# First block of a two-block sequence model on one core: residual held with tokens on partitions, down products that move 512 weight columns, norms by an accumulator and a diagonal matmul

## The reference, cut to what matters

```python
def rmsnorm(x, w):
    xf = x.astype(jnp.float32)
    y = xf * lax.rsqrt(jnp.mean(xf * xf, axis=-1, keepdims=True) + EPS)
    return (y * w.astype(jnp.float32)).astype(x.dtype)

def first_block(x, ...):
    for i in range(DEPTH):                       # DEPTH = 2
        h = rmsnorm(x, norm_mix_pre[i])
        m = ssd_mixer(h, ...) if i == 0 else rglru_mixer(h, ...)    # both end in  y @ w_out (+ b_out)
        x = x + rmsnorm(m, norm_mix_post[i])
        h = rmsnorm(x, norm_ffn_pre[i])
        f = conv_ffn(h, ...)                     # ends in  (gelu(g) * v) @ w_down
        x = x + rmsnorm(f, norm_ffn_post[i])
    return x

def second_block(x, c, ...):
    for l in range(DEPTH):
        h = rms_norm(x, norm1_g[l]) * (1.0 + sc1) + sh1
        ...                                      # attention and delta-rule branches, gates, mlp
```

## Time and profile before

| what | value |
| --- | --- |
| time, median of 3 runs | 1887.17 us (1887.06 to 1896.51) |
| profiled execution, its own time | 1896.59 us |
| its span, first to last instruction | 1894.7 us |
| PE busy, weight loads busy | 96%, 91% of the span |
| DVE busy, ACT busy | 69%, 54% |
| mean granted clock of PE | 0.982 of full speed |

### The profile page before, as it was taken

One profiled execution on the slowest core, in us unless ns is written; L12 is line 12 of the kernel. 1 busy time (PEld: TensorE's weight loads), 2 busy tenths in 40 slices (PEclk: granted clock), 3 DMA queues, 4 the chain that ended last, 5 costly groups with the idle time before them and its releaser, 6 DMA issues. The chain is left out here.

```text
span 1894.7 us, 39895 instructions
## 1 busy us (share of the span) xinstructions
PE 1815.2 (96%) x16265; PEld 1721.7 (91%) x16265; DVE 1316.4 (69%) x2054; ACT 1017.5 (54%) x1542; POOL 29.5 (2%) x48
## 2 busy tenths in 40 slices
PE   6999989999989989999989999999998999999999
PEld 5997879999979979999979998989998999999999
DVE  5857777777778887777767767765557776676554
ACT  5645465555566755555547555454445665454443
POOL 0000000000000000000000001000000000100000
PEclk8999999999999999999989999999999999999999
DMA  7440457667665556656734340345553442044553
GB/s 294 178 177 1 156 184 252 253 263 270 250 255 179 206 181 212 245 227 216 276 110 156 134 156 3 116 153 199 191 187 132 156 150 96 22 158 156 186 191 111
DMA packets 43895, 333.63 MB, mean 176 GB/s; under 512 B 4865, under 2 KB 4993, under 8 KB 5633
## 3 DMA queue, kind: packets, MB, share of 16 engines
q1 hardware_dynamic: 38592, 277.89, 40.7%
q0 software_dynamic: 4608, 50.33, 7.2%
q10 hardware_dynamic: 576, 3.71, 0.5%
HBM read 330.86 MB, written 1.05 MB: 175 GB/s over the span
## 5 line engine op out<-in xcount | busy, mean ns | idle before, releaser
L522 DVE TENSOR_TENSOR w_lo<-raw,w_hi 128x1024 fp32r<-128x1024 f32 x526 | 639.8, 1224 | 389.3 <-ACT w_hi L513 379.3
L513 ACT ACTIVATE w_hi<-raw 128x1024 fp32r<-128x1024 f32 x526 | 554.8, 1060 | 591.7 <-PE unit L544 375.9
L542 PE MATMUL unit<-h_hi,w_hi 128*128 128x256 f32 x2656 | 753.3, 284 | 35.8 <-DVE h_lo L426 14.8
L543 PE MATMUL unit<-h_lo,w_hi 128*128 128x256 f32 x2656 | 745.6, 281 | 0.0
L544 PE MATMUL unit<-h_hi,w_lo 128*128 128x256 f32 x2656 | 745.4, 281 | 0.0
L542 PEld LDWEIGHTS unit<-h_hi,w_hi 128*128 128x128 f32 x2656 | 508.6, 191 | 47.4 <-issue 33.5
L544 PEld LDWEIGHTS unit<-h_hi,w_lo 128*128 128x128 f32 x2656 | 508.3, 191 | 0.0
L543 PEld LDWEIGHTS unit<-h_lo,w_hi 128*128 128x128 f32 x2656 | 507.2, 191 | 0.2
L542 PE MATMUL acc<-mv_hi,w_hi 128*128 128x256 f32 x1360 | 382.3, 281 | 5.9 <-DVE mv_lo L600 3.3
L543 PE MATMUL acc<-mv_lo,w_hi 128*128 128x256 f32 x1360 | 379.1, 279 | 0.0
L544 PE MATMUL acc<-mv_hi,w_lo 128*128 128x256 f32 x1360 | 379.0, 279 | 0.0
(11 more groups left out here) (388 smaller groups left out, 1721.9 us busy)
## 6 DMA issues: line engine op xcount, KB each, us to landing
raw<-w_in SPq DMA_DIRECT2D x263, 1024.0 KB, 4.8
ada_ring<-ada_in POOLq DMA_DIRECT2D x32, 1536.0 KB, 7.5
keep<-gates_in ACTq DMA_DIRECT2D x1, 1280.0 KB, 6.3
par<-par_in ACTq DMA_DIRECT2D x1, 1261.0 KB, 14.5
x<-x_in SPq DMA_DIRECT2D x1, 1024.0 KB, 5.5
out<-x SPq DMA_DIRECT2D x4, 256.0 KB, 2.1
con<-con_in ACTq DMA_DIRECT2D x1, 950.0 KB, 4.9
con<-con_in ACTq DMA_DIRECT2D x1, 130.0 KB, 5.7
```

What stands on the lines that cost most here:

```text
L513: act(half(w_hi, c, k), raw[c % RAW][:, CW // 2 * k:CW // 2 * (k + 1)], ACT.Copy).then_inc(S("high_parts"), 1)
L522: tt(half(w_lo, c, k), raw[c % RAW][:, CW // 2 * k:CW // 2 * (k + 1)], half(w_hi, c, k).bitcast(f32), ALU.subtract).then_inc(S("chunk_spli ...
L542: mm(out, w, m, start=first, stop=False)
L543: mm(out, w, ml, start=False, stop=False)
```

## The change

In the first block `x` is held with 128 tokens on each partition set: `xt` is 2 halves of 128 tokens x 1024 features in the same memory. The down products swap operands: the activations `mv_hi`, `mv_lo` are stationary, 512 weight columns move, and each of the four `acc` banks holds 128 tokens x 512 features (`pe_tokens_down`, 24 matmuls of 512 columns per chunk). The closing chunk runs bank by bank. A norm's sum of squares is then a sum along the free axis, taken by ACT's accumulator output as it squares (`act_post`, `act_pre`); root and scale are one number per partition. The weights of the post norms come as rows, broadcast over partitions, by five DMAs on ACT's queue (`act_rows`) into the unused `h`. To return to features on partitions, DVE scales an identity matrix by the root (`dve_diag`) and PE multiplies 128 x 128 blocks of `xt` by it (`pe_turn`), which turns and scales at once; ACT and DVE make `h_hi` and `h_lo` out of PSUM (`act_turned`, `dve_turned`), or, where `h` itself is needed, by way of it (`dve_turned_exact`). The two blocks of the other product stand together behind the update of the first 128 tokens (`pe_gap`). In the second block's first stage 16 transposes put `x` back to features on partitions. The second block is otherwise unchanged.

```diff
+        def act_post(ac, stage):
+            ...
+            ac.preload_act_table_set(LN_EXP)
+            for b in range(4):
+                m = b // 2
+                if biased:
+                    ac.wait_ge(S("lru_m"), b + 1)
+                else:
+                    closed(ac, stage, b)
+                s = slice(512 * b, 512 * (b + 1))
+                act(spare[:, s], source[:, s], ACT.Square, accum_out=stat(k, 3 * m + b % 2)).then_inc(S("norm_steps"), 1)
+                if b % 2:
+                    ...
+                    act(total, total, ACT.Ln, bias=stat(k, 3 * m + 2), scale=1.0 / D).then_inc(S("norm_steps"), 1)
+                    ac.wait_ge(S("norm_steps"), post_step(k, SUM_AT[b] + 1))
+                    act(total, total, ACT.Exp, scale=-0.5).then_inc(S("norm_steps"), 1)
+
+        def act_pre(ac, name, ready):
+            n = PRE[name]
+            for m in range(2):
+                ready(m)
+                act(spare[:, 1024 * m:1024 * (m + 1)], xt[:, m, :], ACT.Square, accum_out=stat(n, 6 + m)
+                    ).then_inc(S("norm_steps"), 1)
+                ...                       # Ln and Exp on 128x1
+
+        def dve_post(dve, link, stage):
+            ...
+            def product(b):
+                ...
+                if biased:
+                    closed(dve, stage, b)
+                    source = flat(R["m"])[:, 512 * b:512 * (b + 1)]
+                    tt(source, accb[b], rowb(1, b), ALU.add).then_inc(S("lru_m"), 1)
+                    dve.wait_ge(S("lru_m"), b + 1)
+                else:
+                    dve.wait_ge(S("norm_steps"), post_step(k, SUM_AT[b]))
+                ...                       # mw[:, b] = source * weight row; one 128x1 step if b is even
+            def update(b):
+                s = xt[:, b // 2, 512 * (b % 2):512 * (b % 2 + 1)]
+                return stt(s, mw[:, b, :], stat(k, 3 * (b // 2) + 1), s, ALU.mult, ALU.add)
+            product(0)
+            product(1)
+            dve.wait_ge(S("norm_steps"), post_step(k, 4))
+            update(0)
+            update(1).then_inc(S("xt_ready"), 1)
+            product(2)
+            product(3)
+            dve.wait_ge(S("norm_steps"), post_step(k, 8))
+            update(2)
+            update(3).then_inc(S("xt_ready"), 1)
+
+        def dve_diag(dve, name):
+            n = PRE[name]
+            for m in range(2):
+                dve.wait_ge(S("norm_steps"), pre_step(n, 3 * m + 3))
+                ts(diag[:, m, :], ident, stat(n, 6 + m), None, ALU.mult).then_inc(S("norm_factors"), 1)
+
+        def pe_turn(pe, name, n0):
+            ...
+            for m in range(2):
+                pe.wait_ge(S("norm_factors"), 4 * n + m + 1)
+                for t in range(8):
+                    ins = mm(turned(banks, t)[:, P * m:P * (m + 1)], xt[:, m, P * t:P * (t + 1)], diag[:, m, :],
+                             start=True, stop=True, skip_group_check=True)
+                    if m == 1 and t % 2:
+                        ins.then_inc(S("turned"), 1)
+
+        def act_turned(ac, name, n0, weight):
+            ...
+                    ins = act(h_hi[:, t, :], turned(banks, t), ACT.Identity, bias=one("zero"), scale=weight(t))
+        def dve_turned(dve, name, n0, weight):
+            ...
+                    ins = stt(h_lo[:, t, :], turned(banks, t), weight(t), h_hi[:, t, :].bitcast(f32),
+                              ALU.mult, ALU.subtract)
+
+        def pe_tokens_down(pe, c, b, first, last, i=None, chunks=0, downs=0, closing=False):
+            pe.wait_ge(S("mv_ready"), at(i, downs, b + 1))
+            def product(k, m, n, begin, end):
+                s, e = slice(P * m, P * (m + 1)), slice(512 * n, 512 * (n + 1))
+                return three(accb[2 * m + n], mv_hi[:, b % 2, k, s], mv_lo[:, b % 2, k, s], half(w_hi, c, k)[:, e],
+                             half(w_lo, c, k)[:, e], begin, end)
+            if closing:
+                pe.wait_ge(S("chunk_split"), at(i, 2 * chunks, 2 * c + 2))
+                for m in range(2):
+                    for n in range(2):
+                        product(0, m, n, False, False)
+                        ins = product(1, m, n, False, True)
+                        if (m, n) != (1, 1):
+                            ins.then_inc(S("bank_closed"), 1)
+                ins.then_inc(S("half_done"), 2)
+                return
+            ...
 
-        def pe_gap(pe, first, second):
+        def pe_gap(pe, stage, second, name, n0):
 
             n = GAP[second]
-            pe_norm(pe, first)
...
-            pe_ada(pe, n, misc[1])
-
-        def pe_gap_end(pe, second):
-            pe_ada(pe, GAP[second] + 1, accb[0])
+            x_updated(pe, stage)(0)
+            pe_ada(pe, n, accb[0])
+            pe_ada(pe, n + 1, accb[1])
+            pe_turn(pe, name, n0)
...
+            def act_between(stage, name, second, weight):
+                act_post(ac, stage)
+                act_pre(ac, name, x_updated(ac, stage))
+                ahead(act_half, ac, END[stage] - 1, 0)
+                act_turned(ac, name, U0[second], weight)
+                ahead(act_half, ac, END[stage] - 1, 1)
...
+            def dve_between(stage, name, second, weight):
+                dve_post(dve, link, stage)
+                dve_diag(dve, name)
+                dve_turned(dve, name, U0[second], weight)
+                ahead(dve_split, dve, END[stage] - 1)
```

More of the change, by code:

```diff
@@ L398, in pe_norm @@
             n = NI[name]
[L399 to L404 removed]
+            for q in range(4):
+                pe.wait_ge(S("squares"), 4 * n + q + 1)
                 for t in (2 * q, 2 * q + 1):
[L406 removed]
+                    last = mm(misc[0][:, 0:T], ones, h[:, t, :], start=(t == 0), stop=(t == 7))
             last.then_inc(S("square_sums"), 1)
[L409 to L412 removed]
         def x_ready(eng, name):
@@ new lines, in build, with post_step @@
+        rowb = lambda r, b: rows[:, r, 512 * (b % 2):512 * (b % 2 + 1)]
+        spare = flat(h_hi[:, :, :])
+        POST = {"ssd_out": 0, "ffn0": 1, "lru_out": 2, "ffn1": 3}
+        ROWS = {"ssd_out": 0, "ffn0": 1, "lru_out": 2, "lru_bias": 3, "ffn1": 4}
+        SIDE = {"ssd_out": 1, "ffn0": 2, "gates": 3, "lru_out": 5, "ffn1": 6}
+        PRE = {"mix_pre0": 0, "ffn_pre0": 1, "mix_pre1": 2, "ffn_pre1": 3, "pre1_0": 4}
+        STEPS = 8 + 6
+        def post_step(k, j):
+            return 6 + STEPS * k + j
@@ new lines, in pre_step, with stat, act_rows, turned_banks @@
+        def pre_step(n, j):
+            return STEPS * n + j
+        SUM_AT = (1, 2, 5, 6)
+        def stat(n, k):
+            return sums[:, n % 2, k:k + 1]
+        def act_rows(ac, stage):
+            r = 1 if stage == "lru_bias" else 0
+            ac.dma_start(rows[:, r, :], rows_in[:, ROWS[stage], :]).then_inc(S("side_loads"), 16)
+        def turned_banks(n0):
+            return [unit[n0 % 2], unit[(n0 + 1) % 2], misc[0], misc[1]]
+        def turned(banks, t):
+            return banks[t // 2][:, T * (t % 2):T * (t % 2 + 1)]
@@ L466, in dve_post @@
+        def act_turned(ac, name, n0, weight):
+            banks = turned_banks(n0)
             for q in range(4):
-                dve.wait_ge(S("squares"), 4 * NI[name] + q + 1)
+                ac.wait_ge(S("turned"), 4 * PRE[name] + q + 1)
                 for t in (2 * q, 2 * q + 1):
-                    ins = ts(source[:, t, :], source[:, t, :], weight(t), None, ALU.mult)
-                if q == 1 and name in ADDED:
-                    dve_squares(dve, name)
-            link(ins)
-            ahead(dve_half, dve, END[stage] - 1, 0)
@@ L592, in pe_down @@
                 ins.then_inc(S("half_done"), 1)
+        def pe_tokens_down(pe, c, b, first, last, i=None, chunks=0, downs=0, closing=False):
[14 more added lines that the diff above has]
+                return
+            for k in range(2):
+                pe.wait_ge(S("chunk_split"), at(i, 2 * chunks, 2 * c + k + 1))
+                for m in range(2):
+                    for n in range(2):
+                        ins = product(k, m, n, first and k == 0, False)
+                ins.then_inc(S("half_done"), 1)
         def act_moving(ac, b, src, i=None, downs=0):
@@ L906, in act_ssd @@
             rms(1)
+            act_rows(ac, "ssd_out")
             act_out(ac, "ssd_out", ssd_pair, normed, all_ahead=False)
@@ L1385, in act_lru @@
             moving(1)
+            act_rows(ac, "lru_out")
             mult(3)
@@ L1470, in dve_lru @@
             ahead(dve_split, dve, c0 + 13)
-            for t in range(8):
-                if t % 2 == 0:
-                    closed(dve, "lru_out", t // 2)
-                ins = ts(R["m"][:, t, :], acc8[:, t, :], pr("b_out", t), None, ALU.add)
-                if t % 2:
-                    ins.then_inc(S("lru_m"), 1)
         def ada_load(pool, s, block):
@@ L1637, in pe_b2_in @@
                 pe_unit(pe, c0 + j, n0 + j)
+                if l == 0 and j == 1:
+                    pe.wait_ge(S("ada_turned"), 32)
```

(9 more changed lines are left out.)

217 lines of the change are left out of this document (120 added, 97 removed).

## The result

The changed kernel takes 1898.29 us, the median of 15 runs (1893.03 to 1903.37), beside 1887.74 us for the kernel before in the same comparison (15 runs, 1885.65 to 1896.51). The ratio is 1.0044, with a 95% interval of 1.003 to 1.0059. The forecast was 1858. The change was meant to move about 29 us out of the program; it moved some 10 us in.

What follows compares the result with a forecast made beforehand. PE bounds the stages of products; a chain over ACT, PE and DVE, with DVE nearly full, bounds the four passages. -8.5 - 21.8 - 1.0 + 2.0 = -29.3 on the median 1887.2 gave 1858 us, range 1842 to 1880.

Steps and rivals of the forecast that it cites:

- the part on the down products: In `ffn0`, `ffn1` and `ssd_out`, one 512-column matmul at 0.220 us replaces two narrow ones: -8.5 us.
- fixed part: In each down matmul, a cost paid once whatever its width, beside streaming: about 0.006 to 0.010 us, taken as 0.006.
- The rival with 0.28: Down products: a 512-column matmul costs 0.28 us, so the kernel gets slower, 1922 us; chance 0.06.
- The passages: Four stretches from last down to first up matmul get shorter: -5.3, -6.45, -2.8 and -7.2, sum -21.8 us.
- ACT's half split: In the passages, queued between last root and first turned tile: an added wait, in the first from 5.5 to 6.6 us.
- hand-offs: In the passages, passing work between engines and a possibly halved clock: 0.8 us added, 0.9 behind `lru_out`.
- a passage above 13 us: Sign in the profile after: a passage that stays above 13 us would show the forecast wrong.
- Behind `lru_out`: Passage to `ffn1`: DVE free only at 0.75 us, updates end at 10.5, passage 16.45 in place of 19.26: -2.8.
- The first 24 up matmuls: Start of the up stage after a passage: slow before and counted unchanged.
- rival 3: Whole kernel, more than forecast: wide matmuls at 0.215 us and PE kept at upper clock, 1848 or 1843 us; chance 0.20.
- The ends: Program start, from parameters to last tile of `h`: -1.0 us; second block's first stage, 16 transposes: +2.0 us.
- The sum: Whole kernel: down products, passages and ends together, -29.3 us.

Runs made afterwards that it cites:

- the first experiment: Changed kernel with its weight tiles put back to the addresses of the kernel before (padding 76 columns instead of 84); 1867.2 us, ratio 0.9883.
- the second: Kernel before with its weight tiles alone moved by 32 bytes (padding 92 columns instead of 84); 1930.07 us, ratio 1.0225.
- 256 bytes less: Changed kernel with its weight tiles 256 bytes below their place in the kernel before (padding 12 columns); 1866.21 us, ratio 0.9880.
- place 192: Changed kernel with its weight tiles 128 bytes below their place in the kernel before (padding 44 columns); 1891.83 us, ratio 1.0013.

## Why the prediction was wrong

**The step that failed** is in the part on the down products: "the columns that stream are the same, so only what is paid once per matmul can go", with "about 0.006 to 0.010" left per matmul, and with it the unspoken rest of the sum, that every other matmul keeps its spacing. The 0.113 and 0.118 of the earlier trace rows are not streaming and a fixed part: both occur for the same matmul at the same place of the weights, and the spacing changes with where the weights lie against the activations. Behind its first two chunks the stage shown above has 0.1133 before and 0.1187 after. The change moved the weights by 32 bytes. That costs about 30 us (1.0044 less 0.9883, of 1888), spread over the 11,544 matmuls of both blocks that read the weight tiles; the first experiment takes it away and the second brings it into the old kernel. The view that would have warned was at hand: the padding tile ahead of the weights, whose width no part of the change adjusted, though it adds and shortens tiles ahead of it. The range had no room for it, since no rival let a matmul that isn't edited run slower.

**The down products** were sized wrongly apart from that. With the weights in the good place a wide matmul takes 0.229 us on the average, not 0.220. With the pauses between chunks left out, two narrow ones took 0.2273 in `ffn0`, 0.2267 in `ffn1` and 0.2352 in `ssd_out`; a wide one takes 0.2292, 0.2292 and 0.2291. So nothing is gained in place of 8.5 us: `ssd_out` gives 1.2 and the other two take back 1.7. In the kernel as changed, at 0.2333 to 0.2335, they lose 4.6. The term that failed is the fixed part. It rests on the estimate that 256 columns stream in 0.1075, which no run shows; the lowest level seen for such matmuls is 0.1133. Measured against twice that estimate, 0.215, a wide matmul has 0.014 too much and two narrow ones at the lower level 0.012: what is left is not paid once per matmul. The rival with 0.28 is refuted; what else the row holds was not looked into.

**The passages** were right as a sum and in their shape: 9.35, 9.35, 16.45 and 9.75 forecast, 8.71, 8.70, 14.55 and 9.33 measured, 25.4 us in place of 21.8. The chain of the first, in the timeline of the kernel after (start us, duration us):

```profile
241.53 0.60 ACT L502 ACTIVATE h_hi<-acc 128x512 fp32r<-128x512 f32 x1 [0.71 <-PE acc L689]
...
242.00 1.41 DVE L549 TENSOR_TENSOR keep<-acc,h 128x512 f32<-128x512 f32 x2
...
243.44 1.42 DVE L553 SCALAR_TENSOR_TENSOR x<-keep,sums,x 128x512 f32<-128x512 f32 x2
...
244.89 1.06 ACT L516 ACTIVATE h_hi<-x 128x1024 fp32r<-128x1024 f32 x1 [0.45 <-DVE x L553]
...
246.17 1.06 PE L581 MATMUL misc<-rstd,x 128*128 128x128 f32 x8
...
246.40 0.20 ACT L521 ACTIVATE sums<-sums 128x1 f32<-128x1 f32 x1
...
246.50 1.04 ACT L658 ACTIVATE w_hi<-raw 128x1024 fp32r<-128x1024 f32 x1
246.63 0.29 DVE L571 TENSOR_SCALAR rstd<-con,sums 128x128 f32<-128x128 f32 x1 [1.58 <-ACT sums L521]
...
247.06 1.07 PE L581 MATMUL unit<-rstd,x 128*128 128x128 f32 x8
...
247.72 1.93 ACT L592 ACTIVATE h_hi<-unit,con,par 128x256 fp32r<-128x256 f32 x4 [0.18 <-PE unit L581]
...
248.78 1.79 DVE L601 SCALAR_TENSOR_TENSOR h_lo<-unit,par,h_hi 128x256 fp32r<-128x256 f32 x4 [1.86 <-ACT h_hi L592]
```

The last down matmul starts at 241.09. DVE is last at the updates, which end at 244.86, 3.8 after it; 3.9 was forecast. The second root comes at 246.6, 5.5 after, as forecast. From there the prediction had two paths side by side, the identity and the turn to 6.45 and ACT's half split to 6.6, and let the split be last. Measured, the split ends at 247.54, 6.45 after the last down matmul, and the first turned tile can be read at 247.72, 6.63 after: PE is last, by 0.18, and the split is not a wait that is added. PE begins with the second 128 tokens at 247.06, 0.14 after DVE has their identity (246.92) and just as it is through with the first. So the time of this point was right and the engine that sets it was not, in what is nearly a tie. From there to the up stage the trace has 2.08 where 1.95 was counted. The sum without hand-offs, 8.55, comes close to the 8.71 measured; the 0.8 added for hand-offs, which no row gave, was 0.64 too much. (That a passage above 13 us would show the forecast wrong cannot be meant for the one behind `lru_out`, which it put at 16.45.)

Behind `lru_out` DVE came free before the last down matmul, not 0.75 after it as in the earlier trace rows. In the kernel after (start us, duration us):

```profile
651.38 2.35 DVE L667 TENSOR_TENSOR w_lo<-raw,w_hi 128x1024 fp32r<-128x1024 f32 x2
...
662.60 1.42 DVE L553 SCALAR_TENSOR_TENSOR x<-keep,sums,x 128x512 f32<-128x512 f32 x2 [0.78 <-ACT sums L509]
```

That split ends at 653.73, 0.84 before the last matmul, so the updates end 9.45 after it and not 10.5, which is 1.05 of the 1.9 us. From the updates to the up stage the trace has 5.1 and the prediction 5.0 without its hand-offs; the 0.9 that it added for these was again not needed.

**The first 24 up matmuls** were counted unchanged. They gained 6.0 us, for the most part by the clock, as rival 3 had half expected. The windows of the 24 behind the first passage, in the kernel before and then in the kernel after, where the granted clock is the last number but two:

```profile
259.20:264.00 4.80, 4.63 (x24) 4.43 (x25) 4.67 (x8) 1.26 (x2) 0.00 (x0) 0.64 0.75 307
```

```profile
249.80:253.20 3.40, 3.40 (x24) 3.04 (x25) 3.33 (x7) 2.62 (x5) 0.00 (x0) 1.00 0.96 404
```

Before, PE had stood or done small sums for 15 us and began the stage mostly at 1.2 GHz; now its pause is shorter and it begins at 2.4 GHz. Behind all four passages the clock went from 0.55 to 0.70 up to 1.00.

**The ends** came out nearly right, by luck in the first part. The last down matmul of `ssd_out` starts 4.3 us earlier with the weights put back, where 1.0 for the start and 3.1 for the down products had been counted; but the first up matmul of the program already starts 2.8 earlier (24.78 to 21.99), and the down products give 1.2 (192 x 6.1 ns). Two errors cancel. From the 24th up matmul of the second block to its feed-forward part 1.75 us are added, where 2.0 had been counted for the transposes.

**The sum.** With the weights put back the profiled executions differ by 26.9 us (1894.7 to 1867.8) and the medians by 1.17%, 22 us, where 29 were forecast. Of the 26.9 the passages and the 24 matmuls behind them give 31 and the start 2.8. Against that stand the down products with 0.5, the transposes with 1.75, and the up products of `ffn0` and `ffn1` behind their first 24: 0.1152 and 0.1158 us apart in place of 0.1138 and 0.1137, pauses left out, some 5 us. In the new kernel about half of these runs of up matmuls lie at the upper of the two levels, 0.1178, and in the old one nearly all at the lower, 0.1133. What sets the level no run shows.

## What to carry to other kernels

Before timing a change, compare the addresses of the tiles that the matrix engine reads, not only the instructions: a shift of the weights by 32 bytes cost more here (30 us) than four reworked passages gained (25.4). When stages get longer that nothing in the change touches, compare one such stage by windows in both traces; equal counts and clock with a longer stage point to the spacing of the matmuls, and a change of the padding alone tells whether placement is the cause. Take more than one stage and the time of several executions for it, since a stage can be 5 to 6 us longer at the same place (next section). The effect then has to be taken out before the parts of the change are judged.

## What was not expected of the hardware

The spacing of back-to-back 128x128 by 256-column matmuls changed by up to 6% with the distance of the stationary from the moving operand's tiles modulo 256 bytes: in the first layer 176.1 to 177.8 us for the stage of 1536 at 64, 186.5 at 0 and 186.9 at 128. Why a distance should count, the runs don't show: only the place was varied.

At the good place there are still two levels, 0.1133 and 0.1178 us, that hold for long runs of matmuls. The second layer's feed-forward part shows both in kernels that differ only by 32 bytes under all tiles. By windows, the kernel before and then the one with all tiles moved:

```profile
1708.00:1890.80 182.80, 182.80 (x1536) 182.34 (x1536) 100.72 (x107) 81.64 (x96) 0.00 (x0) 0.99 0.45 162
```

```profile
1703.00:1880.00 177.00, 176.33 (x1536) 175.76 (x1536) 101.15 (x108) 81.83 (x96) 0.00 (x0) 0.99 0.47 168
```

Of the seven profiles at relative place 64 three have 182.8 in this stage (before, weights put back, and 256 bytes less) and four 176 to 178; the same stage of the first layer is at the lower level in all seven. The upper level is as slow as place 192, which has 182.8 in both layers. So the length of one stage in one profile does not rank the places; the program's times, of several executions each, do.

The level also changes within a stage, at full clock. In `ffn0` of the kernel with the weights put back the runs of 96 up matmuls between two pauses are 0.1136 and 0.1178 apart in turn. Two neighbouring runs by windows:

```profile
277.55:288.35 10.80, 10.80 (x97) 10.79 (x95) 7.38 (x11) 5.99 (x8) 0.00 (x0) 1.00 0.59 215
295.59:306.78 11.19, 11.19 (x97) 11.19 (x95) 7.33 (x12) 5.98 (x8) 0.00 (x0) 1.00 0.70 243
```

The other two profiles of the new kernel with wide matmuls at place 64 alternate in the same way throughout `ffn0`; in the three of the old kernel all of these runs but one lie at the lower level. There the level goes with the kernel. In the second layer it may change from one execution to the next: the times of the two executions whose second layer is shown above, 1896.59 and 1885.65, are at the two ends of the spread of the old kernel (1885.65 to 1896.51). That is not shown, since each kernel was profiled once. What sets the level stays open.
